# Where 40 modulation blocks stand in a two-block transformer kernel: fewer in the projections, some behind the norms, and constants on multiples of 16 bytes

## The chip, the cores and the metric

One core of one Trainium2 chip runs the whole program in one launch. The time is the device time of that core in microseconds. TensorE is called PE, ScalarE ACT, VectorE DVE, GpSimd POOL, and SyncE SP; SP issues nearly all loads.

## The reference

Everything is fp32, with width 1024, 256 latent tokens x and 256 context tokens. The program holds two transformer blocks. The change touches the first one, which has two layers i = 0, 1 (the second block uses only the constants that are moved):

```
for i in (0, 1):
    mod     = silu(c)     @ w_mod[i] + b_mod[i]      # 1024 -> 6*1024: shift1, scale1, gate1, shift2, scale2, gate2
    mod_ctx = silu(c_ctx) @ w_mod[i] + b_mod[i]      # the same for the context tokens
    h = rms_norm(x, norm1_g[i]) * (1 + scale1) + shift1
    x = x + gate1 * mixer_i(h, h_ctx)                # 0: differential attention, 1: neighbourhood attention
    h = rms_norm(x, norm2_g[i]) * (1 + scale2) + shift2
    x = x + gate2 * (square(relu(h @ w_mlp1[i])) @ w_mlp2[i])
# second block, twice: ffn, hybrid mixer (needs the late constants), memory cross attention, ffn; then a last norm
```

The differential attention has 8 heads with two softmax maps each; the neighbourhood attention has 16 heads on a grid of 4 by 64 tokens with a bias table. Context tokens pass through layer 0 whole, and give only keys and values to layer 1.

## The kernel before

Each product is made of three fp32r passes, because both factors are split into a rounded part and a rest (`passes`, L806: HTl by Wh, HTh by Wl, HTh by Wh). For the weights ACT makes Wh from the loaded block (`prepare`, L1556) and DVE makes Wl (`prepare`, L2082), half a block at a time. Two such halves fit side by side, so the two engines run at most that far ahead of PE.

Weights come as blocks of 1 MB (256 output columns by 1024 rows), in the order of one list (`first_weights`, L590), through a ring of three slots. SP (L2850) issues the load of block i once block i-3 is finished with: a weight block is, when DVE has split both of its halves; a modulation block is, when PE has used it. ACT, DVE and PE then all take the blocks in the order of that list. A block that stands earlier in the list therefore holds a slot that the ones behind it wait for.

The modulation has 48 blocks of 256 columns. The first 8 are done at the start, from rows. The 40 later ones are raw fp32 blocks from the ring: `modulation_block` (L960) does 16 matmul records of 32 by 256 with the two condition vectors as the still operand. They add up in one PSUM bank of their own, `mod_sum`, so that the bank pool A has three banks instead of four while it is in use. When a group of blocks is complete, ACT copies the bank (`copy_group`), PE folds and transposes it (`fold_group`, L771), ACT copies the fold (`copy_folded`) and DVE adds the bias (`add_group`). `gains` (L2150) makes 1 + scale times the norm's gain.

Where the blocks stand now, all in layer 0:

- in the projections, one at the end of each of 18 steps j of `first_layer` (a step is one 128-column tile of q or k: 24 matmuls of the product, `("qs")` for the sum of squares, and a rotation matmul `("qr", j-2)` that waits for `qn_ready`, which DVE gives) and one in each of the two last value steps: 20 in all;
- in the differential attention 20, five in every eight steps (`modulation_step`, L289), the last at step 30.

Groups 1 (16 blocks), 2 (16) and 3 (8) are folded at steps 0, 18 and 34 of the attention. From the MLP of layer 0 on pool A has four banks. In layer 0 the fourth value tile of each half goes to a bank of pool V and is copied out by DVE; in layer 1 all four go to pool A and are copied by ACT.

The constants are one pack of columns per partition. The early part is loaded first; the late part (from "minus", 917 KB) is loaded at ring block 4 into its place in the tile `con`, and starts 8 bytes past a multiple of 16. The scratch tiles of the modulation (`modtwo`, `cT`, `modt`, `fold`) lie in the tile BIG.

Of the kernel before, what the change touches and what calls it, by code (L numbers as in the profile page):

```python
# [45 lines left out]
QK_MOD = 20  # L46
# [52 lines left out]
def constant_pack():  # L99
# [10 lines left out]
    put("ones", np.ones((P, S)))  # L110
# [15 lines left out]
    put("eps", np.full((P, 1), EPS))  # L126

    put("minus", -np.ones((P, P)))
# [11 lines left out]
    qc, kc = p % GRID_W, t % GRID_W  # L140
    start = np.clip(qc - NA_COLS // 2, 0, GRID_W - NA_COLS)
    inside = (kc[None, :] >= start[:, None]) & (kc[None, :] < start[:, None] + NA_COLS)
    back = p // GRID_W * GRID_W + GRID_W - 1 - qc
    put("ncol", np.where(inside, 0.0, NEG)[back])
    half = HEAD // 2
    freq = np.power(np.float32(10000.0), -np.arange(half, dtype=np.float32) * np.float32(2.0 / HEAD)).astype(np.float32)
    put("freq", freq[p % half][:, None])
# [6 lines left out]
LATE_CONST = CONST["minus"][0]  # L154
# [132 lines left out]
def modulation_step(i):  # L287


    places = (0, 1, 3, 5, 6)  # L290
    n = QK_MOD + i // 8 * 5 + (places.index(i % 8) if i % 8 in places else -99)
    return n if QK_MOD <= n < LATER_MOD else None
# [21 lines left out]
def program(nc, I, out):  # L314
    ctx = ExitStack()
    with ctx:
# [92 lines left out]
        modtwo = big(12288, 2, 256)  # L409
        cT = big(12800, KT, 64)  # L410
        fold = BIG[:, 13312:13344]
        modt = big(13344, 2, 64)
# [84 lines left out]
        const_late = sem("const_late")  # L497
        mod_in = [sem(f"mod_in{k}") for k in range(KT)]
# [90 lines left out]

        def first_weights(i):  # L590
            w = I["a_w_qkv" if i == 0 else "b_w_qkv"][0]
            if i == 0:
                later = [columns_of_modulation(m) for m in range(LATER_MOD)]
# [15 lines left out]
            by_columns(I["a_w_o" if i == 0 else "b_w_o"][0], 0, D)  # L609
            if i == 1:  # L610
                late_bias.append(len(blocks))
            n = CHUNK * P
            for c in range(FF1 // n + 1):
                if c < FF1 // n:
                    by_columns(I["w_mlp1"][i], c * n, (c + 1) * n)
                if c:
# [54 lines left out]
        late_bias = []  # L671
# [94 lines left out]
        def _(pe):  # L766
# [342 lines left out]
            def near_attention(tag):  # L1109

                for s in range(len(NEAR_STEPS) + 3):
# [17 lines left out]
                    if s >= 3:  # L1129
# [5 lines left out]
                        for k in range(4):  # L1135
                            for m in range(2):
# [3 lines left out]
                                   v_full if k == 3 and m else None)  # L1140

            def first_layer(i):
                if i == 0:
                    modulation(0)
                else:
                    norm(("n1", i), ALL)
                tiles = qk_tiles(i)
                order = len(tiles)
                for j in range(order + 2):
# [36 lines left out]
                    if i == 0:  # L1186
                        next_modulation(j)
                for n in range(2, 4):
                    values_half(value_tiles(i, 1), CTX_TOKS + LAT_TOKS, 512, n - 2)
                    if i == 0:  # L1190
                        next_modulation(order + n)
# [34 lines left out]
                if i == 0:  # L1226
                    pe.wait_ge(mod_copied, len(MOD_GROUPS))
# [102 lines left out]
            def mixer(l):  # L1330
                pe.wait_ge(const_late, 16)
# [196 lines left out]
        def _(act):  # L1528
# [185 lines left out]
            def near_attention(tag):  # L1714

                for s in range(len(NEAR_STEPS) + 2):
# [6 lines left out]
                    if s >= 2:  # L1723
                        for m in range(2):
                            copy((tag, "T", s - 2, m), near_pt(s - 2)[:, m, :], lambda b: b[:, 0:512])

            def first_layer(i):
# [37 lines left out]
                if i == 0:  # L1765
                    copy_group(1)
# [28 lines left out]
                for c in range(FF1 // P // CHUNK + 1):  # L1795
# [4 lines left out]
                    if c < FF1 // P // CHUNK:  # L1800
                        if c >= 2:
                            act.wait_ge(v_full, V.nth((("dn", i, c - 2), KT - 1)))
                        for j in range(CHUNK):
# [3 lines left out]
                            rounded(HID1h[:, c % 2, j, 0:N], TMP[:, j % 2, 0:N])  # L1807
                    if c == FF1 // P // CHUNK and i == DEPTH - 1:
# [237 lines left out]
        def _(dve):  # L2046
# [257 lines left out]
            def near_attention(tag):  # L2304
# [3 lines left out]
                for s in range(len(NEAR_STEPS) + 3):  # L2308
# [20 lines left out]
                    if s >= 3:  # L2329
# [3 lines left out]
                                lambda b: backward(b[:, 0:P]), quarter(HTl, j)[:, t * P:(t + 1) * P])  # L2333

# [21 lines left out]
            def first_layer(i):  # L2356
# [4 lines left out]
                else:  # L2361
                    gains(1, 0, 1)
# [28 lines left out]
                for _ in range(4 if i else 1):  # L2391
                    prepare()
                if i == 0:
                    copy_in(value_tiles(i, 1)[3][1], Va[:, 3, 512:D], lambda b: b[:, 0:512])
# [12 lines left out]
                else:  # L2407
                    near_attention(("att", i))
                    N, tc = S, LAT
# [3 lines left out]
                for c in range(FF1 // P // CHUNK + 1):  # L2413
# [4 lines left out]
                    if c < FF1 // P // CHUNK:  # L2418
                        for j in range(CHUNK):
# [6 lines left out]
                            rest(HID1h[:, c % 2, j, 0:N], HID1l[:, c % 2, j, 0:N], t)  # L2426
                    if c == FF1 // P // CHUNK and i == DEPTH - 1:
# [463 lines left out]
```

## Time and profile before

| | us |
|---|---|
| time, median of 3 runs | 2628.87 (2625.89 to 2628.97) |
| time of the profiled execution | 2625.73 |
| its span | 2623.9 |
| PE busy | 2502.0 (95%) |
| DVE busy | 1701.4 (65%) |
| ACT busy | 1232.8 (47%) |
| POOL busy | 233.0 (9%) |

The span is what the profile covers; the profiled execution took 1.8 us more than its span. "Busy" is time with an instruction of that engine running, and matmuls overlap, so it says nothing of how fast they run. In the chain of waits each piece is released by the one before it.

### The profile page before, as it was taken

What the parts mean: (1) busy time and instruction counts of PE and PEld (TensorE: products, weight loads), DVE (VectorE), ACT (ScalarE), POOL (GpSimd) and SP (SyncE); (2) the same over time, 40 slices, a digit from 0 to 9 for tenths busy, and PEclk for the clock granted to TensorE, in tenths of its full rate; (3) what the DMA queues carried; (4) which work ended last, traced back from release to release, by engine and by line L of the source; (5) the groups of instructions that cost most, each with busy time, mean ns of one, the idle gap of its engine ahead of it and who ended that gap; (6) DMA issues with size and microseconds to landing.
All of it is one profiled execution on the core that took longest, in us unless ns stands there. A gap on an engine that the chain in (4) does not pass through costs nothing.

```text
span 2623.9 us, 41678 instructions
## 1 busy us (share of the span) xinstructions
PE 2502.0 (95%) x16875; PEld 2218.7 (85%) x16875; DVE 1701.4 (65%) x3155; ACT 1232.8 (47%) x2226; POOL 233.0 (9%) x277
## 2 busy tenths in 40 slices
PE   6999989999989999999999999999999999999998
PEld 4676678888877689999989979899899899798997
DVE  4665855545575666677657677776676577777765
ACT  3444743222355654554444455554544444555543
POOL 1000110000053310000010012000000100120001
PEclk9999999999989999999999999999999999999999
DMA  7665623322334335556564425465765644254654
GB/s 274 206 201 192 215 79 97 97 96 98 99 102 105 81 115 167 170 163 177 169 173 147 154 74 177 129 186 164 205 185 161 171 149 151 87 176 130 177 168 138
DMA packets 497439, 393.74 MB, mean 150 GB/s; under 512 B 26216, under 2 KB 464752, under 8 KB 496352
## 3 DMA queue, kind: packets, MB, share of 16 engines
q1 hardware_dynamic: 494448, 384.92, 48.5%
q0 software_dynamic: 2080, 3.53, 1.1%
q8 instruction: 134, 2.20, 0.4%
q10 hardware_dynamic: 720, 2.62, 0.3%
q14 instruction: 57, 0.47, 0.1%
HBM read 389.99 MB, written 1.05 MB: 149 GB/s over the span
## 4 chain that ended last, share of the span: by engine, by line
PE 85%; DVE 9%; ACT 2%; issue 1%; DMA 1%; POOL 1%; SPq 0%; DVEq 0%; ACTq 0%
PE pv L806 34%; PE pa L806 31%; PE pv L1304 6%; PE pv L771 4%; PE pv L1303 3%; DVE Wl L2082 3%; PE pa L771 2%; PE pa L776 1%; ACT Wh L1556 1%; DMA ring<-in_a_w_qkv_dram 1%; PE pa L960 1%; DVE HTl L2089 0%; POOL BIG L2811 0%; DVE TMP L2173 0%; DVE HTl L2067 0%
## 5 line engine op out<-in xcount | busy, mean ns | idle before, releaser
L2082 DVE TENSOR_TENSOR Wl<-ring,Wh 128x1024 fp32r<-128x1024 f32 (+4 forms) x688 | 758.1, 1142 | 263.1 <-ACT Wh L1556 260.1
L1556 ACT ACTIVATE Wh<-ring 128x1024 fp32r<-128x1024 f32 (+4 forms) x688 | 641.0, 980 | 488.8 <-PE pv L806 322.4
L806 PE MATMUL pa<-HTl,Wh 128*128 128x256 f32 (+1 forms) x1648 | 540.4, 328 | 38.0 <-DVE HTl L2180 24.0
L806 PE MATMUL pv<-HTl,Wh 128*128 128x256 f32 (+1 forms) x1872 | 539.0, 288 | 16.4 <-DVE T L2520 5.9
L806 PE MATMUL pv<-HTh,Wh 128*128 128x256 f32 (+1 forms) x1872 | 537.3, 287 | 0.0
L806 PE MATMUL pv<-HTh,Wl 128*128 128x256 f32 (+1 forms) x1872 | 537.2, 287 | 0.0
L806 PE MATMUL pa<-HTh,Wl 128*128 128x256 f32 (+1 forms) x1648 | 522.2, 317 | 0.0
L806 PE MATMUL pa<-HTh,Wh 128*128 128x256 f32 (+1 forms) x1648 | 521.8, 317 | 0.0
L806 PEld LDWEIGHTS pa<-HTl,Wh 128*128 128x128 f32 x1648 | 320.8, 195 | 72.0 <-issue 45.2
L806 PEld LDWEIGHTS pv<-HTl,Wh 128*128 128x128 f32 x1872 | 359.7, 192 | 22.1 <-issue 12.2
L806 PEld LDWEIGHTS pv<-HTh,Wl 128*128 128x128 f32 x1872 | 359.8, 192 | 2.5
L806 PEld LDWEIGHTS pv<-HTh,Wh 128*128 128x128 f32 x1872 | 359.7, 192 | 2.5
L806 PEld LDWEIGHTS pa<-HTh,Wl 128*128 128x128 f32 x1648 | 320.9, 195 | 20.3 <-issue 1.4
L806 PEld LDWEIGHTS pa<-HTh,Wh 128*128 128x128 f32 x1648 | 320.4, 194 | 18.6
L1304 PE MATMUL pv<-HID,Wh 128*128 128x512 f32 x704 | 246.7, 398 | 0.0
L2750 POOL TENSOR_TENSOR Pb<-Pb 128x256 f32<-128x256 f32 (+1 forms) x60 | 62.5, 1042 | 1454.0 <-ACT Pb L1567 1453.1
L1303 PE MATMUL pv<-HID,Wl 128*128 128x256 f32 x672 | 189.2, 282 | 0.0
L806 PE MATMUL pv<-HID1l,Wh 128*128 128x512 f32 (+1 forms) x512 | 172.0, 336 | 0.0
L806 PE MATMUL pv<-HID1h,Wl 128*128 128x512 f32 (+1 forms) x512 | 172.0, 336 | 0.0
L806 PE MATMUL pv<-HID1h,Wh 128*128 128x512 f32 (+1 forms) x512 | 172.0, 336 | 0.0
L2210 DVE SCALAR_TENSOR_TENSOR XT<-pv,MOD,XT 128x256 f32<-128x256 f32 x216 | 95.6, 479 | 112.0 <-PE pv L806 111.2
L1304 PEld LDWEIGHTS pv<-HID,Wh 128*128 128x128 f32 x704 | 130.4, 188 | 29.3
(288 smaller groups left out, 3301.3 us busy)
## 6 DMA issues: line engine op xcount, KB each, us to landing
ring<-in_ffn_w_gu_dram SPq DMA_DIRECT2D x176, 512.0 KB, 5.1
ring<-in_w_mlp_dram SPq DMA_DIRECT2D x64, 1024.0 KB, 5.3
ring<-in_ffn_w_down_dram SPq DMA_DIRECT2D x64, 704.0 KB, 4.6
ring<-in_w_in_dram SPq DMA_DIRECT2D x42, 1024.0 KB, 5.2
ring<-in_w_mod_dram SPq DMA_DIRECT2D x40, 1024.0 KB, 5.5
ring<-in_a_w_qkv_dram SPq DMA_DIRECT2D x12, 1024.0 KB, 5.3
ring<-in_b_w_qkv_dram SPq DMA_DIRECT2D x12, 1024.0 KB, 5.3
ring<-in_w_out_dram SPq DMA_DIRECT2D x8, 1024.0 KB, 5.1
```

The source lines that it names most:

```text
L771: m = nc.tensor.matmul(o, lhsT=lhsT, rhs=rhs, start=start, stop=stop)
L776: m = nc.tensor.transpose(o, x, C("ident"))
L806: m = nc.tensor.matmul(o, lhsT=x, rhs=y, start=first and j == 0, stop=last and j == 2)
L960: m = nc.tensor.matmul(mod_sum[32 * j:32 * j + 32, 0:256], lhsT=cT[:, k, 30 - 2 * at:62 - 2 * at], rhs=w[:, k, :], start=at == 0 and k < 4 ...
L1303: nc.tensor.matmul(b[:, 0:S], lhsT=wl[:, k, :], rhs=HID2h[:, kk, :], start=False, stop=False)
L1304: m = nc.tensor.matmul(b.rearrange("p (a n) -> p a n", a=2), lhsT=wh[:, k, :], rhs=HID2[:, :, kk, :], start=kk == 0, stop=kk == 2 * half - 1)
L1556: ins = nc.scalar.activation(Wh[rows, p % SPLIT, a:b], ring[rows, i % RING, a:b], ACT.Copy)
L2082: ins = v.tensor_tensor(Wl[rows, p % SPLIT, a:b], ring[rows, i % RING, a:b], Wh[rows, p % SPLIT, a:b].bitcast(F32), ALU.subtract)
L2210: m = v.scalar_tensor_tensor(XT[:, k, half], b[:, at:at + S], MOD[:, i, gate * KT + k, w:w + 1], XT[:, k, half], ALU.mult, ALU.add)
L2750: nc.gpsimd.tensor_tensor(a, a, squares(k)[:, 0:N], ALU.add).then_inc(sum_ready, 1)
```

## The change

Of the 40 later blocks 11 stand in the projections of layer 0 (steps 0, 1, 2, 4, 6, ... 16, 17, placed ahead of the step's wait for `v_free` and `qn_ready`, not at its end), 21 in the differential attention (the last at step 32), two behind each of three norms (norm 2 of layer 0, norm 1 and norm 2 of layer 1) and two behind the second pair of tiles of layer 1's up projection. The weight list follows: in layer 0 m32, m33 stand behind the first two up blocks; in layer 1 m34, m35 behind the first two q blocks (q0, q1), and m36 to m39 behind the first two up blocks (up0, up1), ahead of up2. The groups are now 8, 16, 8, 12 and 4 blocks; group 3 is copied, folded and added in the neighbourhood attention, group 4 in the MLP of layer 1; until then pool A has three banks. The fourth value tile of layer 1 goes to pool V and DVE too. The constants are in three parts, each on a multiple of 16 bytes; the last part (704 KB) is loaded after the last group is added, because the modulation's scratch now lies in its place. "minus" is gone and "ones" is half as wide. `gains` for norm 2 of layer 1 comes after the neighbourhood attention.

```diff
+QK_PLACES = (0, 1, 2, 4, 6, 8, 10, 12, 14, 16, 17)
+QK_MOD = len(QK_PLACES)
+DIFF_MOD = 21
+HOLE_MOD = 2
...
-    put("ones", np.ones((P, S)))
+    put("ones", np.ones((P, P)))
...
-    put("minus", -np.ones((P, P)))
...
-LATE_CONST = CONST["minus"][0]
+LATE_CONST = CONST["ncol"][0]
+LAST_CONST = CONST["halves"][0]
...
-MOD_GROUPS = ((0, FIRST_MOD), (FIRST_MOD, 16), (FIRST_MOD + 16, 16), (FIRST_MOD + 32, 8))
-MOD_COPIED = {18: 2, 32: 3}
-MOD_FOLDED = {0: 1, 18: 2, 34: 3}
-MOD_ADDED = {2: 1, 23: 2, 36: 3}
+AFTER_DIFF = QK_MOD + DIFF_MOD
+AFTER_MLP = AFTER_DIFF + HOLE_MOD
+LAST_MOD = AFTER_MLP + HOLE_MOD
+MOD_GROUPS = ((0, FIRST_MOD), (FIRST_MOD, 16), (FIRST_MOD + 16, 8), (FIRST_MOD + 24, 12), (FIRST_MOD + 36, 4))
+MOD_COPIED = {7: 1, 20: 2}
+MOD_FOLDED = {10: 1, 23: 2}
+MOD_ADDED = {15: 1, 28: 2}
+NEAR_COPIED, NEAR_FOLDED, NEAR_ADDED = 2, 4, 6
...
         def first_weights(i):
...
-                    for src, c in later[2 * n:2 * n + 2] if n < 8 else later[8 + n:9 + n]:
-                        columns(src, c, 256, False)
-                for src, c in later[QK_MOD:]:
-                    columns(src, c, 256, False)
+                    for at, place in enumerate(QK_PLACES):
+                        if n == (place // 2 if place < 16 else place - 8):
+                            modulation_columns(at, at + 1)
+                modulation_columns(QK_MOD, AFTER_DIFF)
+                by_columns(I["a_w_o"][0], 0, D)
             else:
-                by_columns(w, 0, 2 * D)
+                by_columns(w, 0, 512)
+                modulation_columns(AFTER_MLP, LAST_MOD)
+                by_columns(w, 512, 2 * D)
...
+                last_consts.append(len(blocks) + 20)
...
+                elif c == 0:
+                    by_columns(I["w_mlp1"][i], 0, n)
+                    if i:
+                        modulation_columns(LAST_MOD, LATER_MOD)
+                    else:
+                        modulation_columns(AFTER_DIFF, AFTER_MLP)
...
-            return [(V if i == 0 and t == 3 else A, ("v", i, c, t)) for t in range(4)]
+            return [(V if t == 3 else A, ("v", i, c, t)) for t in range(4)]
...
             def first_layer(i):
...
                     norm(("n1", i), ALL)
+                    for n in range(AFTER_MLP, LAST_MOD):
+                        next_modulation(n)
...
+                    if i == 0 and j in QK_PLACES:
+                        next_modulation(QK_PLACES.index(j))
                     if j >= 2 and i == 0:
...
-                    if i == 0:
-                        next_modulation(j)
...
-                    A.width = BANKS
+                    A.width = BANKS - 1
                 norm(("n2", i), tc)
+                first = LAST_MOD if i else AFTER_DIFF
+                for n in range(first, first + HOLE_MOD):
+                    next_modulation(n)
...
                             linear(A, ("up", i), c * CHUNK + j, (0, P), ht(tc), N, c == 0 and j == 0)
+                            if i and (c, j) == (0, 2):
+                                for n in range(LAST_MOD + HOLE_MOD, LATER_MOD):
+                                    next_modulation(n)
+                        if i and c == 1:
+                            fold_group(4)
+                            A.width = BANKS
...
             def mixer(l):
-                pe.wait_ge(const_late, 16)
+                pe.wait_ge(const_last, 16)
...
-                    sp.dma_start(con[:, LATE_CONST:], I["pack"][:, LATE_CONST:CONST_W]).then_inc(const_late, 16)
+                    sp.dma_start(con[:, LATE_CONST:LAST_CONST], I["pack"][:, LATE_CONST:LAST_CONST]).then_inc(const_late, 16)
...
+                if i in last_consts:
+                    sp.wait_ge(mod_added, len(MOD_GROUPS))
+                    sp.dma_start(con[:, LAST_CONST:CONST_W], I["pack"][:, LAST_CONST:CONST_W]).then_inc(const_last, 16)
```

## Rows read from the trace of the kernel before

**Rows 1.** The page: busy time by engine, and the chain that ended last.
```profile
PE 2502.0 (95%) x16875; PEld 2218.7 (85%) x16875; DVE 1701.4 (65%) x3155; ACT 1232.8 (47%) x2226; POOL 233.0 (9%) x277
...
PE 85%; DVE 9%; ACT 2%; issue 1%; DMA 1%; POOL 1%; SPq 0%; DVEq 0%; ACTq 0%
```

**Rows 2.** Chain of waits, q and k steps (start us, us, what).
```profile
70.44 1.76 PE pa L960 x16
72.20 6.53 PE pa L806 x24
...
80.02 1.00 PE pa L960 x16
81.02 5.67 PE pa L806 x24
...
786.84 5.49 PE pa L806 x24
```

**Rows 3.** Window: us, busy of PE, PEld, DVE, ACT, POOL, granted clock, DMA share, GB/s.
```profile
71.00:72.00 1.00, 1.00 (x12) 0.22 (x4) 1.00 (x2) 0.00 (x0) 0.00 (x0) 0.50 0.00 0
```

**Rows 4.** Timeline: start, us, instruction [idle before, releaser]; projections and their end.
```profile
69.77 0.67 PE L771 MATMUL pv<-BIG,con 128*128 128x256 f32 x2 [2.15 <-DVE BIG L2383]
...
225.86 0.69 DVE L2064 COPY BIG<-pv 128x512 f32<-128x512 f32 x1 [20.30 <-PE pv L806]
226.81 1.99 PE L771 MATMUL pv<-BIG 64*128 64x512 f32 x8
```

**Rows 5.** Timeline of the differential attention's end, and the loads' landing (last line).
```profile
310.20 0.37 SPq L2850 DMA_DIRECT2D ring<-in_a_w_o_dram  x1
...
312.61 1.05 ACT L1556 ACTIVATE Wh<-ring 128x1024 fp32r<-128x1024 f32 x1
...
320.85 0.71 PE L771 MATMUL pa<-BIG,PT 128*128 128x128 f32 x4 [1.70 <-ACT PT L1633]
321.40 0.52 PE L771 MATMUL pa<-BIG 128*128 128x16 f32 x4
...
DMA to landing us min/median/max: 5.1/5.2/5.2
```

**Rows 6.** Timeline and chain of waits, first q tiles of layer 1.
```profile
743.79 0.37 SPq L2850 DMA_DIRECT2D ring<-in_b_w_qkv_dram  x1
744.29 2.02 ACT L1556 ACTIVATE Wh<-ring 128x1024 fp32r<-128x1024 f32 x2
...
754.22 5.49 PE pa L806 x24
...
760.36 2.89 PE pa L806 x24
```

**Rows 7.** Timeline of the neighbourhood attention's start.
```profile
870.80 1.99 PE L771 MATMUL pv<-BIG 64*128 64x512 f32 x8 [0.89 <-ACT BIG L1633]
...
873.80 0.42 DVE L2319 CUSTOM_DVE_ANT_0 Lb<-pv,con 128x256 f32<-128x256 f32 x1
```

**Rows 8.** Timeline and chain of waits, norm 2 of layer 1 and first up tiles.
```profile
959.22 25.74 PE pa L806 x192
...
965.34 1.23 DVE L2082 TENSOR_TENSOR Wl<-ring,Wh 128x1024 fp32r<-128x1024 f32 x1
...
966.59 0.37 SPq L2850 DMA_DIRECT2D ring<-in_w_mlp_dram  x1
968.82 2.00 ACT L1556 ACTIVATE Wh<-ring 128x1024 fp32r<-128x1024 f32 x2
969.90 2.36 DVE L2082 TENSOR_TENSOR Wl<-ring,Wh 128x1024 fp32r<-128x1024 f32 x2 [0.34 <-ACT Wh L1556]
```

**Rows 9.** Window of a stretch of back-to-back loads.
```profile
59.00:64.00 5.00, 5.00 (x35) 3.16 (x32) 0.00 (x0) 1.48 (x3) 0.00 (x0) 1.00 1.02 360
```

**Rows 10.** Groups by form: the same DVE instruction with a mask from con, and without.
```profile
L2286 DVE CUSTOM_DVE_ANT_0 Lb<-pv,con 128x256 f32<-128x256 f32 x28 | 11.6, 416 | 0.5 <-PE pv L771 0.4
...
L2286 DVE CUSTOM_DVE_ANT_0 Lb<-pv,RQ 128x256 f32<-128x256 f32 x10 | 4.2, 417 | 0.1
```

More of the change, by code:

```diff
@@ L126, in constant_pack @@
     put("eps", np.full((P, 1), EPS))
-    put("minus", -np.ones((P, P)))
+    half = HEAD // 2
+    freq = np.power(np.float32(10000.0), -np.arange(half, dtype=np.float32) * np.float32(2.0 / HEAD)).astype(np.float32)
+    put("freq", freq[p % half][:, None])
+    put("blank", np.zeros((P, 1)))
+    t = np.arange(S)
+    qc, kc = p % GRID_W, t % GRID_W
+    start = np.clip(qc - NA_COLS // 2, 0, GRID_W - NA_COLS)
+    inside = (kc[None, :] >= start[:, None]) & (kc[None, :] < start[:, None] + NA_COLS)
+    back = p // GRID_W * GRID_W + GRID_W - 1 - qc
+    put("ncol", np.where(inside, 0.0, NEG)[back])
     pb = np.zeros((P, P))
@@ L139, in constant_pack @@
     put("ncausal", np.where(t[None, None, :] <= tok[:, :, None], 0.0, NEG).reshape(P, 2 * S))
[L140 to L147, printed above, removed]
     return np.concatenate(parts, 1).astype(np.float32)
@@ L408, in program, with spare @@
         posi = over("posi", [P, S], where["BIG"] + 4 * 12032, I32)
[L409 to L412, printed above, removed]
+        def spare(at, tiles, width):
+            return con[:, LAST_CONST + at:LAST_CONST + at + tiles * width].rearrange("p (t n) -> p t n", n=width)
+        modtwo = spare(0, 2, 256)
+        cT = spare(512, KT, 64)
+        modt = spare(1024, 2, 64)
+        fold = con[:, LAST_CONST + 1152:LAST_CONST + 1184]
         MODW = over("MODW", [P, 2048], where["SQ"])
@@ L588, in columns_of_modulation, with modulation_columns @@
             return I["w_mod"][layer], n * 256
+        def modulation_columns(m0, m1):
+            for m in range(m0, m1):
+                src, c = columns_of_modulation(m)
+                columns(src, c, 256, False)
         def first_weights(i):
@@ L592, in first_weights @@
             if i == 0:
-                later = [columns_of_modulation(m) for m in range(LATER_MOD)]
                 columns(w, 0, 256)
@@ L1140, in near_attention @@
                                    v_full if k == 3 and m else None)
+                    if s == NEAR_FOLDED:
+                        fold_group(3)
             def first_layer(i):
@@ L1185, in first_layer @@
                         mm(turned_in[:, 0:S], C("pairs"), tiles[j - 2][0][:, LAT], True, True, v_full)
-                    if i == 0:
-                        next_modulation(j)
                 for n in range(2, 4):
                     values_half(value_tiles(i, 1), CTX_TOKS + LAT_TOKS, 512, n - 2)
-                    if i == 0:
-                        next_modulation(order + n)
+                    if i == 0 and order + n in QK_PLACES:
+                        next_modulation(QK_PLACES.index(order + n))
                 if i == 0:
@@ L1807, in first_layer @@
                             rounded(HID1h[:, c % 2, j, 0:N], TMP[:, j % 2, 0:N])
+                        if i and c == 0:
+                            copy_group(4)
+                        if i and c == 1:
+                            copy_folded(4)
                     if c == FF1 // P // CHUNK and i == DEPTH - 1:
@@ L2361, in first_layer @@
                 else:
-                    gains(1, 0, 1)
+                    gains(1, 0)
                     v.tensor_copy(gq[:, 5:6], gq[:, 4:5]).then_inc(am_ready, 1)
@@ L2390, in first_layer @@
                         rotated(tiles[j - 1][0][:, LAT], P, ("qr", i, j - 1), C("cos"), C("sin"))
-                for _ in range(4 if i else 1):
-                    prepare()
+                if i:
+                    for _ in range(3):
+                        prepare()
+                    copy_in(value_tiles(i, 0)[3][1], Va[:, 3, 0:512], lambda b: b[:, 0:512])
+                prepare()
+                copy_in(value_tiles(i, 1)[3][1], Va[:, 3, 512:D], lambda b: b[:, 0:512])
                 if i == 0:
-                    copy_in(value_tiles(i, 1)[3][1], Va[:, 3, 512:D], lambda b: b[:, 0:512])
                     todo = units("diff")
@@ L2408, in first_layer @@
                     near_attention(("att", i))
+                    gains(1, 1)
                     N, tc = S, LAT
@@ L2426, in first_layer @@
                             rest(HID1h[:, c % 2, j, 0:N], HID1l[:, c % 2, j, 0:N], t)
+                        if i and c == 1:
+                            add_group(4)
                     if c == FF1 // P // CHUNK and i == DEPTH - 1:
```

22 lines of the change are left out of this document (12 added, 10 removed).

## The prediction, written before the changed kernel was run

> **What bounds the kernel now.** I read the page first: PE is busy 95% of the span, DVE 65% and ACT 47% [rows 1]. So a change pays only where it takes columns off PE or shortens one of PE's waits, and it costs wherever it makes a new wait. Then I read the chain of waits through the stages that the change touches, with one question each time: is this PE's own work, or another engine's? In the q and k steps of layer 0 it is PE from one end to the other, and each step holds one modulation block: 1.00 us of chain [rows 2]. The timelines then gave the places where PE does wait: 2.15 us at the first rotation [rows 4], 1.70 us near the end of the differential attention [rows 5], and the stretches behind the norms. Last came SP's issues of L2850, because weights and modulation blocks share three slots and their order is changed.
>
> A duration below is of the profiled execution. Its time is 2625.73; the median of the runs shown is 2628.87, so 3.14 is added at the end. A change within 0.2% (5.3 us) can't be told from none.
>
> **Gains in the projections.** Nine of twenty blocks leave.
> - Eight of them stood between products of a PE that never waits there. Each is 1.00 on the chain (80.02 to 81.02). The same 24 matmuls take 5.67 behind a block and 5.49 in layer 1, where there is none [rows 2]; part of the 0.18 may come from the block, so a block is worth 1.00 to 1.18. I take 1.05: 8 x 1.05 = 8.4 (8.0 to 9.4).
> - The ninth stands behind the last value tile, and the attention begins at 226.81. Its first matmul needs that tile's copy by DVE, 225.86 + 0.69 = 226.55, with about 0.05 of handing over [rows 4]. Only 0.2 is gained.
> - The block of step 2 moves ahead of the wait for the rotation's input. PE idles 2.15 there, and then spends 1.76 on the block at a granted clock of 0.50, the lower level [rows 2 to 4]. A block that goes into the idle time leaves the path: 1.76. The product behind it took 6.53 against 5.67 [rows 2], because the clock was still low for a part; a PE that stays busy saves up to 0.86 of that. I take 0.5.
> - 64 KB of constants less before the first weights: at 360 GB/s [rows 9] 0.18; I take 0.15.
>
> Sum of the gains: 8.4 + 0.2 + 1.76 + 0.5 + 0.15 = 11.0.
>
> **End of the differential attention.** There is one block more, at step 32. PE waits 1.70 for ACT right behind that place [rows 5], so I cost the block at 0 (1.07, were the cover gone). The price is in the ring. The first block of `a_w_o` now stands behind one modulation block more. Its slot came free one modulation use before 310.20; now its load goes at 310.20 and lands 5.2 later, at 315.4. ACT wants it at 312.61, in order ahead of the copies that the last attention steps wait for [rows 5]. So ACT stands 2.8 on the chain. The fold that stood at step 34 (0.52 [rows 5]) and its copies leave: -0.5. I take +2.3 (1.0 to 4.5, the upper end with all 2.8, and PE at half its clock behind the wait as in [rows 6]).
>
> **Norm 2 of layer 0.** Its two blocks go into PE's idle time, and the loads behind are wanted much later than they land. I cost this at 0 (-0.5 to 1, a block).
>
> **Norm 1 of layer 1.** The blocks themselves are hidden. But the list is now q0, q1, m34, m35, q2, so that q2's load waits until q1 is split. That moment is SP's issue at 743.79; the load lands 5.2 later, at 749.0. Before, ACT began to split q2 at 744.29 [rows 6]. That makes ACT 4.7 late. The rotation and norm work of DVE stands between, and PE had a wait for Wl there anyway, and after it ran 24 matmuls in 5.49 where the same take 2.89 at full clock [rows 6]. So part of the delay falls on time that was slack or slow already: ACT and DVE do their q and k work while the load flies, and only the split comes after. I take +2.0; the bounds are 0.9 (that slack holds nearly all) and 4.7 (none).
>
> **Start of the neighbourhood attention.** The fourth value tile of layer 1 is now copied by DVE, behind the split at whose end DVE's first attention work stands (873.80), where before ACT did it and PE began at 870.80 [rows 7]. The copy is 0.69 in layer 0 [rows 4]. PE has the S products ready early, so that DVE's copy is what counts: +0.8 (0 to 1.5).
>
> **In the neighbourhood attention** PE folds group 3 (0.5, as [rows 5]), ACT copies it twice, DVE adds it, and pool A has three banks, not four. DVE and PE take turns at the end of the chain there. +1.0 (0.5 to 3, three waits of about the size of the first in [rows 7]).
>
> **Norm 2 of layer 1.** This is the largest cost. Blocks m38, m39 stand behind up1 and ahead of up2 in the list. m36's slot and m37's are free early, but m38 takes up1's slot, which DVE frees at 965.34 + 1.23 = 966.57, and SP issues in order at 966.59. There up2's load went long before. Now three loads of 1 MB go one behind another. The first lands at 966.59 + 5.2 = 971.8; at 360 GB/s [rows 9] 1.049 MB take 2.9, so m39 lands at 974.7, up2 at 977.6. ACT and DVE need 968.82 to 972.26 = 3.4 from the start of a block's split to its end [rows 8]: up2 is ready at 981.0. PE before: 192 matmuls from 959.22 to 984.96 [rows 8], less the last four groups of 24 at 2.89 [rows 6], so up2 began at 973.4. That is +7.6, and the two blocks (2.1 at 1.05) lie within it. PE stands idle for about 5, after which its clock is low, as in [rows 3, 6]: half speed over the first 24 matmuls costs 5.49 - 2.89 = 2.6 at most; I take 2.1. Fold 4 adds 0.5. Sum +10.2 (7.5 to 11.5).
>
> Here a page speaks for less. Back-to-back loads in the trace moved 360 GB/s [rows 9]. The Trainium skill, "DMA: Bandwidth & Descriptors", section "Anatomy of one DMA", gives a load about 2.0 us plus its bytes at 436 GB/s, for the GpSimd path. By that rule the three loads would land 9.2 after 966.59, up2 would be ready at 979.2, this term would be 8.4, and the whole forecast 1.8 lower. The table at the head of the same page gives about 358 GB/s from HBM for one core; by that figure the trace agrees, and nothing moves.
>
> **Alignment.** A DVE instruction that reads its mask from `con`, 8 bytes off, takes 416 ns on 256 columns, and with an operand in RQ 417 [rows 10]. So the constants' place costs DVE nothing and moving it gains 0 (-1 to 1; 28 such instructions of 0.42 are 11.6 in all, so a tenth of them is 1). The last constants, 704 KB, are loaded in the middle of weights that are ahead by then, and the second block needs them hundreds of us later: 0.
>
> **Sum.** Costs 2.3 + 0 + 2.0 + 0.8 + 1.0 + 10.2 = 16.3; less 11.0 is +5.3. 2625.7 + 5.3 = 2631.0 as profiled, and 2634.2 on the scale of the median.
>
> **Rivals.**
> - *The clock holds and the waits are cheap.* Norm 1 costs 0.9, the tail 1.0, the near attention 0.5, its start 0.3, the up tiles 7.6 with no fall of the clock; 10.3 + 0 - 11.0 is about -1: 2627.9. For it: PE, ACT and DVE all have queued work in these stretches, and 5.49 in [rows 6] shows that some of the time given up was slow time. Against: the clock was low behind both pauses of [rows 3, 6]. Chance 0.20.
> - *Every late load is paid in full.* Tail 4.0, norm 1 4.7, start 0.8, near attention 2.5, up tiles 10.3: 22.3 - 11.0 = +11.3, so 2640.2. For it: PE is the bound, and nothing gives a lost microsecond back at 95% [rows 1]; three banks bind more tightly than four. Against: the 2.15 and 0.9 that PE waited before. Chance 0.20.
> - *The other side: the ring is not late.* My reading of who waits for which slot is the whole of the price. If q2's load is given before about 739, so that it lands by 744.29, and up2's before about 964.8 (973.4 less 3.4 and 5.2), the loads come in time, and norm 1 costs 0, the tail 0, and norm 2 only its two blocks and the fold, 2.6. With 0.8 and 1.0 that is 4.4 - 11.0 = -6.6: 2622.3, faster. For it: m36 and m37 are used in a pause, early. Against: SP issues in order, and the issue at 966.59 stands right behind the split's end at 966.57 [rows 8]. Chance 0.20.
> - The forecast itself: 0.40.
>
> The forecast's case lies just at the bound: of its 0.40, 0.24 is slower by over 5.3 and 0.16 within. The cheap case is 0.16 within and 0.04 faster. So faster 0.04 + 0.20 = 0.24; same 0.16 + 0.16 = 0.32; slower 0.24 + 0.20 = 0.44. The forecast's own range is 2630 to 2638. The stated one goes from just under the other side's case to just over the full one, 2621.5 to 2641.5.
>
> **What would show it.** In the trace of the changed kernel: q and k steps without a block that are 1.0 shorter, and no low clock at the first rotation; SP's load of `a_w_o` one modulation block later, and ACT waiting for a DMA near 302 (the stretch comes about 11 earlier); q2's load right behind the split of q1, and ACT waiting for it some 4 us; three loads in one go after up1's split, and PE idle for about 5 before up2 with a granted clock of 0.50 behind. If ACT shows no wait on the ring at the last two, the other side's case holds. If the pause before up2 is there and PE then runs at 1.00, the cheap one does. I am wrong altogether if the q and k steps don't become shorter, which would mean that DVE or ACT takes over as their bound.

## The result: 0.66% slower, three times as much as forecast, and the profile after

The changed kernel takes 2645.02 us (median of 4 runs, 2643.78 to 2646.17), the kernel before 2628.52 (4 runs). The ratio is 1.0066, with a 95% interval of 1.0054 to 1.0078: +16.5 us, where +5.3 was forecast with 2641.5 as the upper end. The profiled execution took 2643.78, 18.05 more than that of before.

On the page PE's busy time is nearly as before (2505.9 against 2502.0 [rows 1]) while the span is 18.1 longer, so most of the loss is waiting; time at the lower clock counts as busy. One engine has more to do though its instructions are the same in number: POOL, 247.5 against 233.0.

```profile
PE 2505.9 (95%) x16879; PEld 2224.2 (84%) x16879; DVE 1707.6 (65%) x3161; ACT 1232.8 (47%) x2226; POOL 247.5 (9%) x277
```

The chain of waits of the changed kernel, stage by stage (start us, us, what). First the products of three q and k steps of layer 0; then the loads that stand on the chain at the end of layer 0's attention, at the first q tiles of layer 1 and behind norm 2 of layer 1; last a piece of the second block's mixer.

```profile
70.54 5.49 PE pa L836 x24
77.32 5.49 PE pa L836 x24
85.30 5.46 PE pa L836 x24
...
299.68 5.07 DMA ring<-in_a_w_o_dram
...
738.30 5.21 DMA ring<-in_b_w_qkv_dram
...
966.46 11.49 DMA ring<-in_w_mlp_dram
...
981.48 13.98 PE pa L836 x96
...
1571.94 1.27 POOL BIG L2867
1573.26 2.64 PE pv L801 x6
1575.89 3.41 PE pa L836 x24
```

Steps are now 6.8 and 8.0 long in turn, and the first product shown, behind the first rotation, runs at full clock (5.49, where it was 6.53 [rows 2]). Three DMAs stand on the chain that weren't there: the late loads of `a_w_o`, of q2 and of the MLP. In the timeline of the changed kernel, the waiting engine at each:

```profile
304.77 1.06 ACT L1598 ACTIVATE Wh<-ring 128x1024 fp32r<-128x1024 f32 x1 [2.51 <-DMA ring<-in_a_w_o_dram]
306.36 1.29 PE L801 MATMUL pa<-BIG,PT 128*128 128x128 f32 x8 [2.61 <-ACT PT L1675]
308.99 2.08 PE L801 MATMUL pa<-BIG,PT 128*128 128x128 f32 x8 [0.91 <-ACT PT L1675]
...
311.85 1.94 PE L990 MATMUL pa<-ring,con 128*32 128x256 f32 x16
...
315.67 0.48 PE L836 MATMUL pv<-HTl,Wh 128*128 128x512 f32 x1
...
743.53 2.00 ACT L1598 ACTIVATE Wh<-ring 128x1024 fp32r<-128x1024 f32 x2 [4.59 <-DMA ring<-in_b_w_qkv_dram]
...
974.99 1.07 PE L990 MATMUL pa<-ring,con 128*32 128x256 f32 x16 [2.54 <-DMA ring<-in_w_mod_dram]
...
981.48 0.58 PE L836 MATMUL pa<-HTl,Wh 128*128 128x256 f32 x1 [5.41 <-DVE Wl L2130]
```

These answer to rows 5, 6 and 8. The granted clock was at the lower level from 307.2 to 314.1, behind the wait of 2.61. So PE took the block at step 32 in 1.94, and not hidden in a wait, and the eight matmuls ahead of it in 2.08; eight such matmuls take 1.16 in the kernel before.

At the start of the neighbourhood attention PE waits too. Before, it idled 0.89 there for ACT [rows 7]; in the changed kernel:

```profile
870.17 4.93 PE L801 MATMUL pv<-BIG 64*128 64x512 f32 x12 [4.40 <-DVE BIG L2112]
```

Since the order of the products is the same in all kernels, one number per stage tells where the time goes: how much later (or earlier, below 0) the same matmul starts than in the kernel before. The first line is its time there. "after" is the changed kernel; the others are the experiments below. The difference between neighbouring columns is the cost of the stage between them.

```
before     224   293   335   690   824   935   990  1019  1070  1510  2240  2610
after    -12.2 -12.0  -5.8  -5.7  -4.2  -1.2  10.9  10.9  11.2  11.2  14.9  18.2
a_off8   -12.0 -11.8  -5.3  -5.1  -2.9   1.0  12.4  12.4  15.4  15.5  15.5  15.3
a_tail   -10.2 -10.0  -8.3  -8.8  -6.9  -3.7   7.8   7.8  10.9  10.9  14.6  17.8
a_fold   -11.8 -12.1  -7.6  -7.9  -6.4  -2.1   9.2   9.2  12.2  12.2  15.7  18.8
a_mlp4   -12.0 -11.8  -6.3  -1.7   0.8   3.5   3.3   3.3   6.4   6.4  10.0  13.3
a_holes  -13.0 -12.8  -6.1  -3.4  -5.7  -2.4  -2.7  -2.7  -2.5  -2.4   1.3   4.7
best     -12.1 -12.4 -11.7  -9.3  -8.8  -6.0  -6.3  -6.3  -4.5  -4.7  -4.8  -5.1
best_on16 -10.5 -10.7 -10.3 -7.8 -10.3  -7.0  -7.3  -7.3  -7.1  -7.0  -3.3   0.0
b_on16     2.1   2.1   2.1   2.1   2.2   2.6   2.4   2.4   5.5   5.5   9.1  12.8
b_off4    -0.2  -0.2  -0.2  -0.1  -0.1   0.3   0.2   0.2   3.2   3.3   3.3   3.3
b_off12   -1.6  -1.6  -1.6  -1.7  -4.9  -5.0  -5.2  -5.2  -2.1  -1.9   1.8   5.4
```

The line "after" reads: projections -12.2; differential attention up to 293 +0.2, its last part +6.2; norm 1 and the q and k tiles of layer 1 +1.5; neighbourhood attention +3.0; norm 2 and first up tiles +12.1; the rest of that MLP +0.3; and 7.0 in the second block, in which the change had no cost in my sum.

What is different there is POOL. Groups of POOL by form, of the kernel before (the forecast used none of these rows) and of the changed kernel: the second block multiplies by a mask in `con` (first two lines of each), the neighbourhood attention adds another one.

```profile
L2816 POOL TENSOR_TENSOR TMP<-TMP,con 128x512 f32<-128x512 f32 x10 | 11.2, 1121 | 9.0 <-ACT TMP L1945 8.9
L2811 POOL TENSOR_TENSOR BIG<-BIG,con 128x512 f32<-128x512 f32 x10 | 10.9, 1092 | 388.8 <-DVE BIG L2611 388.8
...
L2707 POOL TENSOR_TENSOR HTf<-HTf,con 128x256 f32<-128x256 f32 x8 | 4.9, 635 | 0.0
```

```profile
L2872 POOL TENSOR_TENSOR TMP<-TMP,con 128x512 f32<-128x512 f32 x10 | 13.1, 1307 | 10.2 <-ACT TMP L1993 10.2
L2867 POOL TENSOR_TENSOR BIG<-BIG,con 128x512 f32<-128x512 f32 x10 | 12.7, 1272 | 387.7 <-DVE BIG L2667 387.7
...
L2763 POOL TENSOR_TENSOR HTf<-HTf,con 128x256 f32<-128x256 f32 x8 | 5.7, 729 | 0.0
```

On a multiple of 16 bytes the constant makes the POOL instruction of 128x512 0.18 longer and that of 128x256 0.09. The kind that works in BIG (L2867, L2811 before) stands on the chain of waits, ten times in the changed kernel and eight times before. 20 times 0.18 and 32 times 0.09 are 6.5 of POOL's 14.5; the rest was not explained.

### The profile page after: what moved, and what is told of

Same layout as the page of the kernel before. It is cut to its first block, busy times and chain, and to the rows that moved or that the text cites. A ratio compares the mean times of both kernels' runs of the same rounds, so it can differ in the third digit from the quotient of the medians.

```text
span 2642.0 us, 41700 instructions
## 1 busy us (share of the span) xinstructions
PE 2505.9 (95%) x16879; PEld 2224.2 (84%) x16879; DVE 1707.6 (65%) x3161; ACT 1232.8 (47%) x2226; POOL 247.5 (9%) x277
## 4 chain that ended last, share of the span: by engine, by line
PE 83%; DVE 9%; ACT 3%; DMA 2%; issue 2%; POOL 1%; SPq 0%; DVEq 0%; ACTq 0%; POOLq 0%
PE pv L836 34%; PE pa L836 30%; PE pv L1346 6%; PE pv L801 5%; PE pv L1345 3%; DVE Wl L2130 3%; PE pa L801 2%; ACT Wh L1598 1%; DMA ring<-in_a_w_qkv_dram 1%; PE pa L806 1%; PE pa L990 1%; DVE TMP L2221 1%; DVE HTl L2228 1%; POOL BIG L2867 0%; DMA ring<-in_w_mlp_dram 0%
## 5 line engine op out<-in xcount | busy, mean ns | idle before, releaser
L836 PEld LDWEIGHTS pa<-HTh,Wh 128*128 128x128 f32 x1648 | 319.8, 194 | 18.2
```

The source lines that it names most:

```text
L836: m = nc.tensor.matmul(o, lhsT=x, rhs=y, start=first and j == 0, stop=last and j == 2)
```

## Experiments

Names with a_ start from the changed kernel, with b_ from the kernel before. The runs of the kernel before beside them had a median of 2626.36 for a_off8, b_on16, a_tail and a_mlp4, of 2627.65 for a_fold, a_holes, best and b_off4, and of 2626.95 for b_off12 and best_on16. The profiled executions carry some us of chance (two places of it are shown below), so a small difference in one stage is no finding by itself, and a claim on the total goes by the intervals.

**a_off8: the changed kernel, its constants off the multiples of 16.**

```diff
-    put("blank", np.zeros((P, 1)))
+    put("blank", np.zeros((P, 3)))
```

> The changed kernel with two blank columns ahead of its later constants, so that they stand 8 bytes past a multiple of 16 as before; nothing else differs. Theory C (the constants' place): GpSimd's multiplication of 128x512 by the mask in con, 1.27 us in the changed kernel and 1.09 before, goes back to 1.09, the pauses of PE in the second block's mixers become as short as before, and the clock doesn't fall in them: some 6.9 us less in the second block and up to 1 in the neighbourhood attention, 2645.0 becomes 2637 to 2639. Theory D (the clock's falls come with the moment at which a pause lies, and the whole second block has moved by 11 us): the second block keeps most of its 6.9, the time stays within 2 of 2645. If the GpSimd durations don't change, C falls in any case.

Measured 2640.00 (ratio to before 1.0050, 1.0037 to 1.0062). A group of POOL of this kernel:

```profile
L2867 POOL TENSOR_TENSOR BIG<-BIG,con 128x512 f32<-128x512 f32 x10 | 10.9, 1093 | 388.9 <-DVE BIG L2667 388.9
```

The whole loss of the second block is gone: from 15.5 at 1510 to 15.3 at 2610, where "after" goes from 11.2 to 18.2. So theory C holds in the stage. The total shows it only in part: by the ratios it is 0.16% below the changed kernel, the intervals overlap, and the median lies outside the ranges of both theories. In the profiled executions the 7.2 gained in the second block are less 2.8 lost between 1019 and 1070, a place that comes up again below, and 1.5 that this kernel was later at 990.

**b_on16: the kernel before, with the constants on multiples of 16.**

```diff
+    put("blank", np.zeros((P, 2)))
     put("minus", -np.ones((P, P)))
```

> The kernel before with two blank columns ahead of its later constants, so that they stand on multiples of 16 bytes; nothing else differs. Theory C: GpSimd's multiplication by the mask takes 1.27 instead of 1.09, and the kernel becomes 5 to 8 us slower, 2634 to 2637, nearly all of it in the second block's mixers, where the clock falls. Theory D: no change beyond 1.5 us.

Measured 2637.18 (1.0037, 1.0023 to 1.0051), +10.8 on the kernel before, just above theory C's range. Of the profiled 12.8 only the 7.3 in the second block can be laid on the masks. Neither theory expected the rest. 3.1 are lost between 1019 and 1070, and b_off4 below loses 3.0 there too, though POOL's product with the mixers' mask is as short in it as before. 2.1 are lost by 224, where the lower level was granted for 6.8 at the first rotation and for 3.4 before. No POOL instruction stands behind those.

Why 7 when ten times 0.18 is 1.8? The chain has the answer; one pause stands here for the others. Here the kernel before, then a_off8:

```profile
1560.12 1.10 POOL BIG L2811
1561.27 1.56 PE pv L771 x6
1562.83 2.87 PE pa L806 x24
```

```profile
1567.45 1.10 POOL BIG L2867
1568.59 1.56 PE pv L801 x6
1570.16 2.88 PE pa L836 x24
```

In the changed kernel the same three pieces took 1.27, 2.64 and 3.41 (above). The pause became longer and the granted clock was lower behind it. Here are windows of the changed kernel at that place and at the next one, then the kernel before at both (columns as in [rows 3]; the clock is the third number from the end).

```profile
1572.00:1575.00 3.00, 1.74 (x5) 1.45 (x6) 1.08 (x4) 0.42 (x1) 2.43 (x2) 0.76 0.00 0
1575.00:1578.00 3.00, 3.00 (x18) 2.82 (x17) 2.07 (x3) 0.00 (x0) 0.00 (x0) 0.67 0.00 0
1625.00:1628.00 3.00, 3.00 (x15) 3.00 (x16) 2.93 (x5) 2.98 (x6) 2.54 (x4) 0.50 0.91 304
```

```profile
1564.00:1567.00 3.00, 3.00 (x24) 2.89 (x23) 2.22 (x3) 0.90 (x2) 0.28 (x1) 1.00 0.06 7
1612.00:1615.00 3.00, 3.00 (x27) 3.00 (x26) 2.97 (x4) 2.97 (x6) 2.56 (x4) 1.00 0.77 267
```

So at most 1.8 is the instructions, and about 5 the lower clock level (1.2 of 2.4 GHz) that PE was granted behind slightly longer pauses. The granted clock of the other kernels agrees. Behind 1510 each of the eight kernels in which POOL's product with the mixers' mask takes 1.27 has four stretches of 3.4 at the lower level that the kernel before lacks (in the changed kernel from 1573.6, 1624.8, 2351.8 and 2420.1). The three in which it takes 1.09 (a_off8, best, b_off4) have none of them. At half speed such a stretch costs up to 1.7.

**a_tail: the list order at the end of the attention.**

```diff
-                modulation_columns(QK_MOD, AFTER_DIFF)
-                by_columns(I["a_w_o"][0], 0, D)
+                modulation_columns(QK_MOD, AFTER_DIFF - 1)
+                by_columns(I["a_w_o"][0], 0, 256)
+                modulation_columns(AFTER_DIFF - 1, AFTER_DIFF)
+                by_columns(I["a_w_o"][0], 256, D)
```

> The changed kernel with the first block of a_w_o one place earlier in the list, ahead of the last modulation block of the differential attention; the blocks' places on TensorE are the same. Theory R (the ring): ScalarE's 2.51 us of waiting for that load go, and with it the low clock behind (6.8 us of it), so 4 to 6 us less: 2639 to 2641. Theory X (the extra block at step 32 and its ordering cost it): at most 1.5 less, 2643.5 to 2645.

Measured 2641.37 (1.0055, 1.0043 to 1.0068), 0.11% below the changed kernel by the ratios; the intervals overlap. The stage is clear: from 293 to 335 it loses 1.7, "after" 6.2. In the timeline of this kernel:

```profile
304.14 1.05 ACT L1600 ACTIVATE Wh<-ring 128x1024 fp32r<-128x1024 f32 x1
...
309.89 1.07 PE L992 MATMUL pa<-ring,con 128*32 128x256 f32 x16
...
311.26 1.06 ACT L1600 ACTIVATE Wh<-ring 128x1024 fp32r<-128x1024 f32 x1 [0.57 <-DMA ring<-in_a_w_o_dram]
...
313.11 0.48 PE L838 MATMUL pv<-HTl,Wh 128*128 128x512 f32 x1
```

ACT's 2.51 of waiting is gone: at 304.14 it begins the first block of `a_w_o` without a wait, and the 0.57 at 311.26 is for the second block. The block at step 32 takes 1.07 instead of 1.94. Theory R holds in the stage: one place in the list is worth 4.5 there (the total is 0.4 above R's range). Most of it is not in the total, because this kernel gained 2.0 less by 224 and lost 3.1 between 1019 and 1070.

**a_mlp4: blocks m36 to m39 out of layer 1.** In the list and on PE they are replaced by one block each behind the up tiles of chunks 1 to 4 of layer 0, and the groups are 8, 16, 8, 16:

```diff
+                    if i == 0 and c <= MLP_MOD:
+                        modulation_columns(IN_MLP + c - 1, IN_MLP + c)
...
-                            if i and (c, j) == (0, 2):
-                                for n in range(LAST_MOD + HOLE_MOD, LATER_MOD):
+                            if i == 0 and 1 <= c <= MLP_MOD and j == 2:
+                                next_modulation(IN_MLP + c - 1)
```

> The changed kernel with the four blocks of norm 2 and the up projection of layer 1 (m36 to m39) taken away from there, and four blocks instead behind up tiles of layer 0's MLP, in chunks 1 to 4; the last two groups become one of 16 and fold in the neighbourhood attention, and pool A has four banks behind that. Theory R: the stretch of norm 2 of layer 1 gives back its 12.0 (three loads in one go ahead of up2, idle PE, low clock), and four blocks of 1.05 come in layer 0 where loads have time: 7.8 less, 2636 to 2639. Rival B (three banks and the fold in the MLP cost it, not the loads): the same total gain but PE without an idle stretch ahead of up2 in the changed kernel; that is excluded by the changed kernel's chain, which shows 11.49 of DMA there. Rival P (placing raw blocks between the MLP's weight blocks costs as much in layer 0, 3 us each): no gain, 2644 to 2648.

Measured 2639.81 (1.0047, 1.0035 to 1.0060), 0.8 above theory R's range. From 935 to 990 it goes from 3.5 to 3.3, "after" from -1.2 to 10.9: without the four blocks, their loads and their fold, the 12.1 of norm 2 are gone. That it is the loads is told by the 11.49 of DMA on the changed kernel's chain, and by a_holes below. Four blocks in layer 0 cost 4.6 (-6.3 to -1.7), more than the 4.2 expected; chain of this kernel:

```profile
438.39 21.76 PE pa L838 x96
461.15 22.03 PE pv L838 x96
```

438.39 + 21.76 = 460.15, so the block is 1.00, and the product behind is 0.27 longer than the 21.76 of a stretch without a block: 1.27 in all.

**a_fold: group 2 folded at step 26, not 23.**

```diff
-MOD_FOLDED = {10: 1, 23: 2}
-MOD_ADDED = {15: 1, 28: 2}
+MOD_FOLDED = {10: 1, 26: 2}
+MOD_ADDED = {15: 1, 31: 2}
```

> The changed kernel with group 2 folded at step 26 of the differential attention and added at step 31, in place of 23 and 28. In the changed kernel TensorE waits 1.31 for ScalarE's copy of the fold ahead of a head's transposes and loses 2.1 in all between the steps 22 and 27. Theory F (the fold's place, where only two banks are free for it): 1.5 to 2.1 less. Rival (the extra modulation block in the same steps costs it): within 0.5 of the changed kernel.

Measured 2643.62 (1.0059, 1.0046 to 1.0072). The total tells nothing. In the table it loses 4.5 from 293 to 335, "after" 6.2. The other profiles show that this is the fold's place: by the measure of the table, between 291 and 305 the five kernels with the fold at step 23 (after, a_off8, a_tail, a_mlp4, a_holes) lose 1.9 each, and the three with it at step 26 (a_fold, best, best_on16) 0.5. So the place is worth about 1.5.

**a_holes: where the blocks stand in the list.** Two blocks go to layer 0's MLP, as in a_mlp4, and two each stand behind the norms of layer 1; the groups are 8, 16, 8, 14 and 2.

```diff
-                by_columns(w, 0, 512)
+                by_columns(w, 0, 256)
                 modulation_columns(AFTER_MLP, LAST_MOD)
-                by_columns(w, 512, 2 * D)
+                by_columns(w, 256, 2 * D)
...
+                    by_columns(I["w_mlp1"][i], 0, n // 2)
+                    modulation_columns(LAST_MOD, LAST_MOD + 1)
+                    by_columns(I["w_mlp1"][i], n // 2, n)
+                    modulation_columns(LAST_MOD + 1, LATER_MOD)
```

> The changed kernel with only the blocks m34 to m39 and their places in the list changed as said for the run best: two in layer 0's MLP, two behind each norm of layer 1, none behind the up tiles. Theory R: norm 1 gives back its 1.6 and norm 2 and the up tiles 11 of their 12; two blocks in the MLP cost 2.5: 10 less than the changed kernel, 7 to 8 over the kernel before on the same chip. Rival H: only 3 to 5 less than the changed kernel.

Measured 2631.53 (11 runs; 1.0015, 1.0006 to 1.0024), 0.51% below the changed kernel by the ratios. Norm 2 costs -0.3 instead of 12.1, norm 1 and the q and k tiles -2.3 instead of 1.5, two blocks in the MLP 2.7. So two blocks behind norm 2 are free, once the loads of the weights behind them don't wait for them. The run changes both the number of blocks there (two, not four) and their place in the list, and does not part the two. More came back than R expected (13.5 in the profiled executions against 10): norm 2 gave 12.4 where R had 11, and norm 1 gave 3.8 where R had 1.6. But norm 1's stage is no sure reading, since it costs 0.5 in best, which has the same edit there, and b_off12, which has none, gains 3.2 in it.

**best: all of it together.** The edits of a_off8, a_tail, a_fold and a_holes.

> The changed kernel with all that the runs so far point to: constants 8 bytes past a multiple of 16, the first block of a_w_o ahead of the last modulation block in the list, group 2 folded at step 26 of the attention (not 23), two of the later blocks in layer 0's MLP, two behind norm 1 and two behind norm 2 of layer 1, with the list q0, m36, m37, q1 and up0, m38, up1, m39, up2. Theory R: the ring no longer comes late; the gain of the projections (12) stays less 2.5 for the two blocks in the MLP, some 2.5 in the neighbourhood attention and 1 for the last fold: 4 to 7 below the kernel before, 2619.5 to 2622.5. Rival H (a block in a pause costs its time whether or not its load is there, at half clock 1.9 each): four such blocks take back 7.6, no gain, 2626 to 2630.

Measured 2619.85 (2617.23 to 2620.43; ratio 0.9967, 0.9955 to 0.9980): 7.8 faster than the kernel before and 25 than the changed kernel. It is the fastest of all. Timeline of PE behind the norm 2 of layer 1:

```profile
948.75 1.07 PE L999 MATMUL pa<-ring,con 128*32 128x256 f32 x16
950.09 1.07 PE L999 MATMUL pa<-ring,con 128*32 128x256 f32 x16 [0.27 <-DMA ring<-in_w_mod_dram]
953.26 0.55 PE L845 MATMUL pa<-HTl,Wh 128*128 128x256 f32 x1 [2.09 <-DVE HTl L2236]
```

Both blocks lie in a pause that ends with DVE's HTl, as it did before, and they run at the full level (1.07 each, not the 1.9 of rival H).

**best_on16: best, but with the constants on multiples of 16** (without the edit of a_off8).

> The run best with its constants back on multiples of 16 bytes, nothing else. Theory C: the same 5 to 11 us are lost as when the kernel before was given them, so 2626 to 2631. Rival (the cost only comes with the order of the other two kernels): within 2 of best, 2618 to 2622.

Measured 2626.61 (11 runs; 0.9995, 0.9986 to 1.0005), 0.28% above best by the ratios. The constants' place spends nearly all that the order of the blocks gains. Its price on the total agrees in three pairs: 0.28% here, 0.27% in b_off12 and 0.37% in b_on16, each against the same order with quick places.

**b_off4 and b_off12: which places are slow.** The kernel before, with blank columns so that the mask of the mixers stands 4 (12) bytes past a multiple of 16 and the neighbourhood's column mask 12 (4) past:

```diff
+    put("blank", np.zeros((P, 3)))     # b_off12: 1
     put("minus", -np.ones((P, P)))
...
+    put("blank2", np.zeros((P, 2)))
     put("ncol", np.where(inside, 0.0, NEG)[back])
```

> The kernel before with its later constants at other places: the mask that GpSimd multiplies by 4 bytes past a multiple of 16, the neighbourhood's column mask 12 past. Theory C1 (a multiple of 16 is the slow case, any other is quick): GpSimd's 128x512 product with the mask takes 1.09, the 128x256 one with the column mask 0.63, and the time is that of the kernel before within 1.5. Rival C2 (8 past is the only quick place): 1.27 or more and 0.73, and 5 to 11 more, as with multiples of 16.

> The kernel before with the two masks' places exchanged against the run b_off4: the mask that GpSimd multiplies by stands 12 bytes past a multiple of 16, the neighbourhood's column mask 4 past. So far 0 past is slow for both, 8 past quick for both; 4 past was quick for the first (1.09) and 12 past slow for the second (0.73). Theory P (the place decides: 4 and 8 past are quick, 0 and 12 slow): the first takes 1.27, the second 0.63, and the time is 5 to 11 over the kernel before. Rival T (the instruction decides: the second is quick at 8 alone, the first everywhere but at 0): 1.09 and 0.73, and the time is within 1.5 of the kernel before.

Measured 2628.97 (11 runs, 2622.54 to 2632.81; 1.0001, 0.9992 to 1.0010) and 2634.09 (9 runs; 1.0027, 1.0017 to 1.0036). Groups of POOL, b_off4 and then b_off12:

```profile
L2813 POOL TENSOR_TENSOR BIG<-BIG,con 128x512 f32<-128x512 f32 x10 | 10.9, 1093 | 388.8 <-DVE BIG L2613 388.8
L2709 POOL TENSOR_TENSOR HTf<-HTf,con 128x256 f32<-128x256 f32 x8 | 5.7, 730 | 0.0
```

```profile
L2813 POOL TENSOR_TENSOR BIG<-BIG,con 128x512 f32<-128x512 f32 x10 | 12.7, 1267 | 389.3 <-DVE BIG L2613 389.3
L2709 POOL TENSOR_TENSOR HTf<-HTf,con 128x256 f32<-128x256 f32 x8 | 4.9, 635 | 0.0
```

C1 and C2 both fell; theory P holds: with the masks exchanged the durations exchange too. 0 and 12 past are slow, 4 and 8 quick, for both instructions. The table agrees over all kernels: from 1510 to 2610, the eight with the mixers' mask at 0 or 12 (after, a_tail, a_fold, a_mlp4, a_holes, best_on16, b_on16, b_off12) lose 6.6 to 7.3, and the three with it at 4 or 8 (a_off8, best, b_off4) -0.4 to 0.0.

**A place where only the clock decides.** b_off4 and the kernel before run within 0.3 of each other up to 1019, and 3.2 apart at 1070. Their chains there, the kernel before first:

```profile
1025.42 11.93 PE pa L806 x96
...
1051.42 3.69 PE pa L771 x16
```

```profile
1025.58 13.34 PE pa L808 x96
...
1052.98 5.38 PE pa L773 x16
```

Windows of both, the kernel before first, show the granted clock (third from the end):

```profile
1024.00:1030.00 6.00, 6.00 (x44) 6.00 (x43) 2.31 (x7) 0.69 (x2) 0.00 (x0) 0.81 0.54 175
```

```profile
1024.00:1030.00 6.00, 6.00 (x31) 6.00 (x30) 2.04 (x6) 0.00 (x0) 0.00 (x0) 0.53 0.55 175
```

The work is the same, but the lower clock level was granted for longer. Seven of the eleven kernels lose 3.0 to 3.1 there, best 1.8, three 0.3 or less, and it goes with none of the edits. So the total of one such kernel carries a few us that its edit did not cause.

## Why the prediction was wrong

The direction and the mechanism in the ring were right; the sum was 12.8 short of the profiled difference (5.3 against 18.1). By its own steps:

- **Projections, -11.0: measured -12.2.** A block was worth the upper bound, 1.18: two steps' products are 5.46 + 5.49, and the distance grew by 1.2 for each block. Some 0.8 had come by time 55, ahead of the first of these steps, where the lower level was granted for 6.8 and not 10.2. The block ahead of the rotation did leave the path, and the clock did not fall there. That was in part luck: in a_tail and best_on16, which have the same blocks there, the lower level was granted for 3.4 behind that place, and they had gained 10.2 and 10.5 by 224.
- **Alignment, 0 (-1 to 1): measured +7.0 in the second block. This is the step that failed.** "So the constants' place costs DVE nothing" was true [rows 10] and it was the wrong engine. The same constants are read by POOL. 20 of its instructions with the mixers' mask take 0.18 longer, ten of them on the chain, and behind the longer pauses the lower clock was granted for four more stretches of 3.4. The bounds were made from DVE rows alone; no POOL row was read. The direct part, up to 1.8, would have left the bound of 1 too.
- **End of the differential attention, +2.3 (1.0 to 4.5): measured +6.2.** ACT waited 2.51 where I had 2.8, so the ring was read rightly. What I mis-sized is what follows: "PE waits 1.70 for ACT right behind that place, so I cost the block at 0" failed, since with the clock at the lower level the block took 1.94 on the chain, and the matmuls ahead of it took 2.08 where they take 1.16 at the full one. a_tail puts 4.5 on the late load and all that follows. The place of group 2's fold is about 1.5 more (a_fold); I had only counted the fold that left.
- **Norm 2 of layer 0, 0: measured +0.1.**
- **Norm 1 of layer 1, +2.0: measured +1.5.** q2's load went out at 738.30 behind the split of q1, ACT waited 4.59, and most of it was given back, as argued. The clock gave back a part: between 725 and 790 its mean was 0.95, and 0.87 in the kernel before. Chance in this stage is as large as the term.
- **Neighbourhood attention, +0.8 + 1.0: measured +3.0.** "PE has the S products ready early" failed: the S products wait for DVE's copy of the fourth value tile, and DVE takes that copy (0.68 from 869.23) only behind the split of the next weight block (2.36 from 866.95). PE idled 4.40 for it (0.89 before), and DVE's first attention work, at 872.09, was 2.5 later than the kernel's lead of 4.2 would have it. Most of this came back while the kernel before ran at the lower level for 6.8 from 876.1 and the changed one only for 3.4 from 870.4: at 884 the net cost was 0.8, the forecast number by luck. The other 2.2 came from 885 on. In b_on16, which has the slower masks alone, the stage costs 0.4; what is left between the fold and the three banks stays open. All eight kernels with this order (the changed one, those with a_, best, best_on16) have the wait of 4.40, and the stage costs them 2.7 to 4.3.
- **Norm 2 of layer 1, +10.2 (7.5 to 11.5): measured +12.1.** I had up2 ready at 981.0; it was 981.48, in a kernel that by then ran 1.2 ahead, so 1.7 later than worked out. PE's last wait was 5.41, and the clock was at the lower level from 976.3 to 986.5. SP gave the three loads at 965.42, 965.83 and 966.46, and they landed 5.2, 9.1 and 11.49 after that, so the last at 977.95: 12.5 after the first was given, where 5.2 + 2 x 2.9 is 11.0. While all three were under way the windows show 351 to 365 GB/s:

```profile
968.00:972.00 4.00, 4.00 (x41) 3.66 (x44) 0.00 (x0) 0.00 (x0) 0.00 (x0) 1.00 1.09 365
972.00:976.00 4.00, 1.46 (x27) 0.42 (x16) 0.00 (x0) 0.00 (x0) 0.00 (x0) 1.00 1.10 351
```

  The rule of the Trainium skill, "DMA: Bandwidth & Descriptors", section "Anatomy of one DMA", gave an estimate of 9.2 for the three; the page has it for the GpSimd path. These loads, which SP issued, took 12.5, so for them the measurement decides.

The rival "every late load is paid in full" was nearest for layers 0 and 1, +11.3 against +11.2 at 1070, though by errors of both signs. The other side's rival fell: SP issued in order, and both loads came late.

## What to carry to other kernels

Before an operand's place is called harmless, read the rows of every engine that reads it, and bound the cost with the slowest one. In a ring, a filler block costs what its slot makes late, and not its own time: norm 2's stage cost 12.1 or -0.3 (after, a_holes) by how many blocks stood there and where in the list. Price a longer pause of PE at the clock behind it as well; here that was about 5 of 7 us.

## What the runs showed of the hardware

- A POOL TENSOR_TENSOR on fp32 whose second operand starts 0 or 12 bytes past a multiple of 16 took 1.27 us for 128x512 and 0.73 for 128x256 (b_off12 and b_off4 for 12, the changed kernel for 0); 4 or 8 past, 1.09 and 0.64. Other engines' instructions with the same constants did not change (DVE's with a mask took 416 ns in the kernel before [rows 10], 418 in the changed one, 417 in b_on16, 416 in b_off4 and b_off12). Why, and whether the first operand's place counts too, was not tried.
- The granted clock at a given pause can differ between two kernels that run within 0.3 us of each other up to it. 3 us of the profiled span came and went that way (b_off4 against the kernel before).
- The modulation blocks inside the pause behind norm 2 ran at the full level (1.07 each, best), and so did one behind a wait of 2.54 (974.99, changed kernel). The one at step 32 of the changed kernel, some 5 us after a wait of 2.61, ran at the lower level (1.94).
- 1-MB loads that SP issued one behind another landed 5.2, 9.1 and 11.49 after their issue, at 351 to 365 GB/s (changed kernel).
